# A hybrid decoder block on eight cores: barriers between four stages taken out, loads and first chunks of the next stage issued among the last steps of the one before

## The reference

```python
h = rmsnorm(x, attn_norm_g)
c_q, c_kv, k_pe, dq, dk, dv, ga, gb = split(h @ w_in)
o_a = mla_attention(c_q, c_kv, k_pe, ...) @ w_o_mla      # 8 heads, dense causal, low rank q and kv, RoPE
o_b = dilated_attention(dq, dk, dv) @ w_o_dil            # 3 groups (window, dilation) = (128,1),(512,4),(2048,16), 4 heads each
x = x + (sigmoid(ga + b_a) * o_a + sigmoid(gb + b_b) * o_b) @ w_out
h2 = rmsnorm(x, ffn_norm_g)
u = causal_dwconv(h2 @ w_up, conv_w, conv_b)             # width 3, 2 * 5504 features
x = x + (silu(u_gate) * u_up) @ w_down
out = rmsnorm(x, final_norm_g)
```

## Time and profile before

| | |
|---|---|
| median of 3 runs | 4726.3 us (4726.19 to 4990.38) |
| profiled execution | 4733.6 us, span of its slowest core (6) 4732.1 us |
| spans of the eight cores | 4712.8 to 4732.1 us |
| PE busy | 4335.3 us (92%) |
| VectorE, ACT busy | 1826.8 us (39%), 1532.8 us (32%) |
| DMA | 802 MB, mean 170 GB/s |

### The profile page before, as it was taken

The page is one execution under the profiler, slowest core; times in us unless marked ns, Lnnn a source line. Parts: engine busy times, 40 slices in busy tenths (PEclk is TensorE's granted clock), DMA queues, the critical chain, the costliest instruction groups (busy, mean ns, idle before and its releaser), DMA issues.

```text
span 4732.1 us, 79343 instructions; the slowest of 8 cores (4712.8 to 4732.1 us)
## 1 busy us (share of the span) xinstructions
PE 4335.3 (92%) x29258; PEld 2556.6 (54%) x29456; DVE 1826.8 (39%) x3318; ACT 1532.8 (32%) x2872; POOL 133.0 (3%) x223
## 2 busy tenths in 40 slices
PE   4979999964979899789999999999999999999998
PEld 3856666632545555445555555555555555555554
DVE  4733333200221322314752267224752267323762
ACT  3636666630111212213431244113431144113330
POOL 0000000000000000000000000000000000000000
PEclk8989999987989999789999999999999999999999
DMA  8648797889898442076556655676666655676555
GB/s 238 224 77 105 106 108 106 108 174 134 155 163 168 116 109 66 5 226 198 189 199 218 219 187 187 203 239 197 188 199 210 220 187 188 201 236 197 187 176 169
DMA packets 193662, 802.49 MB, mean 170 GB/s; under 512 B 23348, under 2 KB 44324, under 8 KB 177380
## 3 DMA queue, kind: packets, MB, share of 16 engines
q1 hardware_dynamic: 164148, 607.49, 40.1%
q0 software_dynamic: 29136, 189.92, 24.6%
HBM read 882.30 MB, written 138.96 MB: 216 GB/s over the span
## 4 chain that ended last, share of the span: by engine, by line
PE 84%; DMA 6%; DVE 3%; ACT 2%; issue 2%; another core or an unknown queue 2%; SPq 1%; DVEq 0%; POOL 0%; ACTq 0%; POOLq 0%
PE wide L260 76%; PE bank L260 7%; DMA cs<-cosT 2%; DMA h<-Hs 1%; DMA w<-w_gate_bf 1%; SPq L74 1%; ACT pt L269 1%; DVE tm L275 1%; DMA wuq<-w_uq 1%; DMA wd<-w_dn_bf 0%; ACT pt L536 0%; DVE zacc L272 0%; DVE on L484 0%; ACT zacc L269 0%
## 5 line engine op out<-in xcount | busy, mean ns | idle before, releaser
L260 PE MATMUL wide<-h,w 128*128 128x410 bf16 (+2 forms) x11297 | 2069.9, 341 | 161.9 <-DMA h<-Hs 149.6
L260 PEld LDWEIGHTS wide<-h,w 128*128 128x128 bf16 x11360 | 1094.4, 98 | 1091.9 <-issue 188.5
L260 PE MATMUL wide<-hid,wd 128*128 128x410 bf16 x3440 | 603.3, 336 | 1.4 <-DMA wd<-w_dn_bf 1.4
L275 DVE SCALAR_TENSOR_TENSOR ac<-u,vecs_sb,ac 128x410 f32<-128x410 f32 x860 | 551.5, 642 | 45.6 <-DVE ac L275 0.9
L269 ACT ACTIVATE ac<-u,vecs_sb 128x410 f32<-128x410 f32 x430 | 313.8, 730 | 539.9 <-DVE u L272 539.9
L260 PEld LDWEIGHTS wide<-hid,wd 128*128 128x128 bf16 x3440 | 334.8, 97 | 269.1 <-issue 2.2
L272 DVE TENSOR_TENSOR u<-wide,rs 128x410 f32<-128x410 f32 x430 | 251.0, 584 | 300.9 <-PE wide L260 244.5
L536 ACT ACTIVATE pt<-wide,vecs_sb 128x1024 bf16<-128x1024 f32 x256 | 284.4, 1114 | 211.9 <-PE wide L260 202.7
L269 ACT ACTIVATE sq<-x 128x410 f32<-128x410 f32 (+1 forms) x166 | 138.5, 834 | 554.6 <-DVE x L272 525.6
L260 PE MATMUL wide<-qp,kpe 128*128 128x512 bf16 (+4 forms) x953 | 306.4, 339 | 9.8 <-DVE vh L447 4.2
L272 DVE TENSOR_TENSOR x<-wide,x 128x410 f32<-128x410 f32 x160 | 93.5, 584 | 476.8 <-PE wide L260 476.8
(11 more groups left out here) (146 smaller groups left out, 3076.6 us busy)
## 6 DMA issues: line engine op xcount, KB each, us to landing
w<-w_up_bf SPq DMA_DIRECT2D x430, 512.0 KB, 3.4
w<-w_gate_bf SPq DMA_DIRECT2D x160, 512.0 KB, 4.1
h<-Hs SPq DMA_DIRECT2D x64, 1024.0 KB, 14.8
wd<-w_dn_bf SPq DMA_DIRECT2D x80, 704.0 KB, 4.3
wd<-w_dn_bf SPq DMA_DIRECT2D x80, 672.0 KB, 4.2
w_up_bf<-w_up POOLq DMA_DIRECT2D x43, 1024.0 KB, 13.9
w<-w_out_bf SPq DMA_DIRECT2D x80, 512.0 KB, 4.2
x<-xT SPq DMA_DIRECT2D x16, 2048.0 KB, 10.2
```

Source lines behind the costliest of these rows:

```text
L260: P.op("pe", lambda E: E.matmul(out_ap, lhsT=lhsT_ap, rhs=rhs_ap, start=start, stop=stop, **kw), reads=reads, writes=[out_T])
L275: P.op("dve", lambda E: E.scalar_tensor_tensor(out=out_ap, in0=in0, scalar=scalar, in1=in1, op0=op0, op1=op1), reads=reads, writes=[out_T])
```

## The change

The four stages become one phase: `end_phase` is called once, at the end. For that each SBUF tile gets a fixed place, and a "generation" (its stage). When a tile is first touched it waits for the readers and writers of those earlier tiles that lie where it lies (`touch`). Tensors in DRAM that one stage writes and another reads (`Hs`, `MOs` by head, the cast weights by name) are tracked too (`Dram`). Then work is moved:

- Stage 1: w_lat tiles 6, 4, 5 first; 0 to 3 one each after j = 0 to 3. Stage 2's wukv and its tables csq are sent at j = 13, wuq at j = 15. wukv and csq lie in free space, wuq in the place of x tile 1.
- Stage 2: the tails of stage 1's last chunk run after the first six of head 0's units. Fill also runs whenever the next product opens the output banks (`opens`). Casts: 68 here, not 63.
- Stage 3 becomes a generator that yields after each projection group. h tiles 0 and 1 and five weights are sent at the start of head 6, the bias table and four weights at that of head 7. Its first eight groups (j = 0 to 2) are head 7's fill, and one more runs with each pending step after head 7. Evictions of these use one bank (6), later three. Casts: two after each j from 3 on, 37 in all.
- Stage 4: mo is two tiles (heads of the latent attention, of the dilated one). Twelve gate groups (`gate`, `PRE`) are issued in pairs between the last seven steps of stage 3; h is sent before them. Gate outputs have 16 tiles, not 4. The rest is as before.

The functions of stage 3 (`chunk`, `quad`, `halo`, `finish`) move up in the file, with their text unchanged but for names. The core of the diff:

```diff
+    def touch(self, deps):
+        assert not self.dead, "tile used again where a later one lies: " + self.name
+        if not self.seen:
+            self.seen = True
+            for o in self.over:
+                o.dead = True
+                if o.lw is not None:
+                    deps.add(o.lw)
+                deps.update(o.rd)
...
+class Dram:
+    def __init__(self):
+        self.lws = []
+
+    def on_read(self, o, deps):
+        deps.update(self.lws)
+
+    def on_write(self, o, deps):
+        self.lws.append(o)
...
-            dst, src = casts[cast_i[0]]
-            P.dma("pool", dst.rearrange("a p m -> (a p) m"), src.rearrange("a p m -> (a p) m"), key="cast%d" % (cast_i[0] % 4),
-                  xdeps=[after])
+            dst, src, nm = casts[cast_i[0]]
+            P.dma("pool", dst.rearrange("a p m -> (a p) m"), src.rearrange("a p m -> (a p) m"), writes=[bf_M[nm]],
+                  key="cast_" + nm, xdeps=[after])
...
+    def T_at(name, t, lo, hi, gen):
+        over = [o for o in known if o.gen < gen and o.lo < hi and lo < o.hi]
+        n = T(name, t, lo, hi, gen, over)
+        known.append(n)
+        return n
...
+    la = Space(1, 3072, 44064)
...
+    s1 = Space(1, 60480, 212832)
...
+    s2 = Space(2, 44064, 143200)
...
+    s3z = Space(3, 143200, 212832)
+    w3 = [s3z("w3_%d" % i, [128, 16, 128], BF16) for i in range(5)]
+    hr3 = Ring([s3z("h3_%d" % i, [128, 16, 512], BF16) for i in range(3)])
+    s3a = Space(3, 3072, 44064)
...
+    NC, NT4, PRE = 410, 5, 12
+    w4 = [T_at("w4_%d" % i, t.t, t.lo, t.hi, 4) for i, t in enumerate(w3[0:7])]
+    s4 = Space(4, 163680, 180064)
+    sgr4 = Ring([s4("sg4_%d" % i, [128, NC], BF16) for i in range(PRE + 4)])
...
+    for i in (6, 4, 5):
+        wl_load(i)
...
+            if j < 4:
+                wl_load(j, [P.ops[-1]])
+            if j == NT1 - 3:
+                P.dma("pool", wukv_all.t[:], w_ukv_d.rearrange("o p (k m) -> p o k m", m=128), writes=[wukv_all], key="wukv")
+                P.dma("sp", csq.t[0:64, :], cos_d[:, HALO0:SEQ], writes=[csq], key="cosq")
+                P.dma("sp", csq.t[64:128, :], sin_d[:, HALO0:SEQ], writes=[csq], key="sinq")
+            if j == NT1 - 1:
+                P.dma("pool", wuq_all.t[:], w_uq_d.rearrange("o p (k m) -> p o k m", m=128), writes=[wuq_all], key="wuq")
...
+                    if j >= 3:
+                        cast_some(cast_i[0] + 2, P.ops[-1])
...
+        for u in units[0:6]:
+            u()
+        for f in older:
+            f()
+        for u in units[6:]:
             u()
...
+        ncast_p2 = len(casts) * 65 // 100
         for h in range(8):
             Kh, Vh, qn, qp = cur
-            nxt, fill = head_units(h + 1, Ring([banks[6]])) if h < 7 else (None, [])
+            if h < 7:
+                nxt, fill = head_units(h + 1, Ring([banks[6]]))
+            else:
+                nxt, fill = None, [lambda: next(gen3) for _ in range(8)]
+                load_bias()
+                for kg in WORDER[5:]:
+                    wt0[kg] = load_w(0, *kg)
+            if h == 6:
+                hts.extend([load_h(0), load_h(1)])
+                for kg in WORDER[0:5]:
+                    wt0[kg] = load_w(0, *kg)
+            nfill = len(fill)
             stepn, total = 0, 55
...
+                opens = len(pend) > LAG and pend[0][0]
+                if fill and (opens or len(fill) * total > nfill * (total - stepn)):
                     fill.pop(0)()
                 while len(pend) > LAG:
-                    pend.pop(0)()
+                    pend.pop(0)[1]()
...
+            pend.pop(0)[1]()
+            next(gen3)
...
+        pb3[0] = Ring(banks[4:7])
+        for _ in gen3:
+            pass
...
+        def load_mo(it):
+            for i, (a, b) in enumerate(((0, 8), (8, 12))):
+                P.dma("pool", mo.t[:, a:b, :], MOs[a:b, :, it * NC:(it + 1) * NC].rearrange("c p t -> p c t"),
+                      reads=MOs_M[a:b], writes=[moc[i]], key="mo4_%d" % i)
...
+        def gate(m, half):
+            wg, sg = wload("w_gate", 16 * half + m, 16), sgr.next()
+            b = linear(wg, 16, hsc, lambda kc: hs.t[:, kc, :])
+            act(sg, sg.t[:], b.t[:, 0:NC], AF.Sigmoid, [b, vecs], bias=vcol(V_BGATE + half * 16 + m))
+            return sg
...
+        load_h(0)
+        P.op("dve", lambda E: E.memset(ones_f.t[:], 1.0), writes=[ones_f])
+        P.op("dve", lambda E: E.memset(carry.t[:], 0.0), writes=[carry])
+        pre = []
+        run_steps()
+        while steps:
+            for _ in range(2):
+                if len(pre) < PRE:
+                    pre.append(gate(len(pre) // 2, len(pre) % 2))
+            run_steps()
+        while len(pre) < PRE:
+            pre.append(gate(len(pre) // 2, len(pre) % 2))
+        load_mo(0)
         load_x(0)
+        pb4[0] = Ring(banks[0:6])
         for it in range(NT4):
...
+                for half, (nm, kcn, mobase) in enumerate((("w_omla", 8, 0), ("w_odil", 4, 8))):
+                    sg, tm = pre.pop(0) if pre else gate(m, half), tmr.next()
+                    wo = wload(nm, m, kcn)
```

More of the change, by code:

```diff
@@ L201, in build_program @@
     MOs = dram("MOs", [12, 128, NEXT], BF16, "Internal")
-    Hs_T = T("Hs", None)
-    bf = {}
+    Hs_M = Dram()
+    MOs_M = [Dram() for _ in range(12)]
+    bf, bf_M = {}, {}
     casts = []
@@ L210, in build_program @@
         for i in range(0, n, step):
-            casts.append((bf[nm][i:min(i + step, n)], src[i:min(i + step, n)]))
+            casts.append((bf[nm][i:min(i + step, n)], src[i:min(i + step, n)], nm))
+        bf_M[nm] = Dram()
     cast_i = [0]
@@ new lines, in build_program @@
+    cqn = la("cqn", [128, 4, NEXT], BF16)
+    ckvn = la("ckvn", [128, 2, SEQ], BF16)
+    kpe = la("kpe", [128, SEQ], BF16)
+    s1 = Space(1, 60480, 212832)
+    x_1 = s1("x1_1", [128, 16, TW], F32)
+    sqr1 = Ring([s1("sq1_%d" % i, [128, 16, TW], BF16) for i in range(2)])
+    x_2 = s1("x1_2", [128, 16, TW], F32)
+    x_0 = s1("x1_0", [128, 16, TW], F32)
+    xr1 = Ring([x_0, x_1, x_2])
+    wl = [s1("wl%d" % i, [128, 16, 128], BF16) for i in range(7)]
+    raw1 = Ring([s1("raw1_%d" % i, [128, 4, TW], F32) for i in range(2)])
@@ new lines, in build_program @@
+    sqs1 = Ring([s1("sqs1_%d" % i, [128, 4, TW], BF16) for i in range(2)])
+    csr1 = Ring([s1("cs1_%d" % i, [128, TW], F32) for i in range(4)])
+    tmr1 = Ring([s1("tm1_%d" % i, [128, TW], F32) for i in range(2)])
+    rsr1 = Ring([s1("rs1_%d" % i, [128, TW], F32) for i in range(5)])
+    hr1 = Ring([s1("h1_%d" % i, [128, 16, TW], BF16) for i in range(4)])
+    VP = 136
+    s2 = Space(2, 44064, 143200)
+    wukv_all = s2("wukv", [128, 16, 2, 128], BF16)
+    csq = s2("csq", [128, NEXT], F32)
@@ new lines, in build_program @@
+    dor.append(s3c("dout1", [128, 1025], BF16))
+    dor = Ring(dor)
+    Uacc = s3c("uacc", [128, NEXT], F32)
+    Zacc = s3c("zacc", [128, NEXT], F32)
+    ptr3 = Ring([s3c("pt3_%d" % i, [128, 1024], BF16) for i in range(2)])
+    tmr3 = Ring([s3c("tm3_%d" % i, [128, 1024], F32) for i in range(2)])
+    qT += [s3c("dq%d" % g, [128, NEXT], BF16) for g in (1, 2)]
+    Vt += [s3c("vt1", [128, 20, 128], BF16), vt2]
+    qTj = [[part("dq%d_%d" % (g, j), qT[g]) for j in range(8)] for g in range(3)]
@@ new lines, in build_program @@
+    mo = s4("mo4", [128, 12, NC], BF16)
+    moc = [part("mo4a", mo), part("mo4b", mo)]
+    w4.append(s4("w4_7", [128, 16, 128], BF16))
+    wr4 = Ring(w4)
+    s4 = Space(4, 196448, 212832)
+    hs = s4("h4", [128, 16, NC], BF16)
+    hsc = [part("h4c%d" % k, hs) for k in range(16)]
+    carry = s4("carry4", [128, 86, 2], F32)
+    ones_f = s4("ones4", [128, 128], F32)
+    s4 = Space(4, 11264, 44064)
+    xs = s4("x4", [128, 16, NC], F32)
+    xsc = [part("x4c%d" % k, xs) for k in range(16)]
```

540 lines of the change are left out of this document (241 added, 299 removed).

## The result

The change makes the kernel faster by 2.3%: the ratio of the times after to before is 0.9774, with an interval of 0.9751 to 0.9798. Its executions took 4616.1 to 4622.7 us, against 4726.2 and 4726.3 before. By the ratio that is 107 us (95 to 118) where 196 were forecast, and the time lies above the range of 4480 to 4600.

A forecast was written before the change was run, and what follows sets the result against it. Bound: PE, nearly full in stage 4, with idle time elsewhere, including waits for h tiles. 6 + 23 + 12 + 108.5 + 28.7 - 16 + 34 = 196 us off the median 4726.3 gives 4530; range 4480 to 4600.

The forecast's parts named there:

- A: Start of stage 1: four w_lat loads moved later leave less before the first x; 6 us gain (0 to 12).
- B: Stage 1 to 2: wukv, csq and wuq sent early, query units start sooner; 23 us gain (20 to 30).
- C: Stage 2 output-bank openings: a fill unit of the next head covers PE's waits; 12 us gain (0 to 20).
- D: Stage 2 to 3 and slot s = 0: early loads and eight chunks in head 7; 108.5 us gain.
- Rival 3: Stage 2 to 3: something behind the barrier already held the order, tiles arrive no faster; 82 us off, 4644; chance 0.05.
- E: Stage 3 slot s = 1: fewer casts make it cost what s = 2 does; 28.7 us gain (20 to 32).
- G: Stage 3 to 4: twelve gate groups and one omla group done earlier; 34 us gain (21 to 36).
- F: Heads 6, 7 and s = 0: moved DMA work makes h tiles late; 16 us loss (0 to 60).
- sign of failure: Head 7 fill chunks wait for DMA, or h waits total over 60 us: where the forecast fails first.
- rival 4: Head 7: each of eight chunks waits 28 us behind casts, attention too; 225 us lost, slower at 4755; chance 0.03.
- Rival 1: Slot s = 0: the DMA debt is not paid, late h tiles cost 60 us; 109.5 off, 4617; chance 0.12.
- equal turns between queues: Engines alternate queues per packet: tiles beside casts take about twice their time, F nothing, sum 4514; as rival 4488, chance 0.08.

The follow-up runs named there:

- no_opens: The changed kernel without the extra fill unit where the output banks open; one run took 4613.2 us.
- os_on_pool: The changed kernel with the stores of the latent attention's outputs issued by POOL, not SP; ratio 0.9732, fastest run 4590.5 us.
- before_new_casts: The kernel before, barriers left in, with the cast plan of the changed kernel alone; ratio 0.9852, fastest 4652.6 us.
- spread_casts: The changed kernel with 48 casts by head 5's end, none in heads 6 and 7, then 10, 13, 17, 17 by slot; ratio 0.9634, fastest 4548.6 us.
- gates_behind: The changed kernel with sixteen gate groups, four behind the last output step, weights sent before the last stores, and another cast plan; ratio 0.9615, fastest 4536.2 us.
- no_casts_67: The changed kernel with 50 casts by head 5's end, none in heads 6 and 7, three after each j from 3; ratio 0.9676, fastest 4570.0 us.

## Why the prediction was right and wrong

**Right.** *A and B* were forecast at 29 us and brought 21 and 25 on cores 6 and 2 (18 and 29 on cores 0 and 4). The rows at 270.50 and 275.66 show that the tails of j = 15 pause PE for 2.1 and 3.9 us; no wait for wukv or wuq is left. *C* was 12; the waits of no_opens put it at 11. *D*, behind stage 2: s = 0 was to cost from j = 3 on what s = 2 costs, 161.7 us. To the marks of the table, which leave out about 7 us of that stretch, it is 153.9 and 154.3, 97% of it busy. Rival 3 (what stood behind the barrier holds the order anyway) is out. The chunks in stage 2 cost about what was charged, 25.7 us for ten at a price of 30.2. *E* was 28.7 and is 31.2 (core 6), and s = 1, 2 and 3 agree within 3 us. *G* goes as it was told, with a wait between the last output step and the first `mo` group. It was to be 20 us to the first `odil` group; it was 24.7 (1917.99 to 1942.70). The `omla` group that was to run in between itself came 18.2 us late: its tile stands behind the stores on SP, and the forecast had not followed SP's list to it. In size G is smaller than told: 25.6 us on core 6 and 11 to 24 on the other cores read, for 34.

**Wrong: F, the DMA debt.** It was to cost 16 us, as late h tiles in s = 0. That engines would be full from head 6 on was right (0.98 to 1.00). But s = 0 came out clean, and the price was paid in stage 2, at 72 to 82 us. By steps:

- Heads 6 and 7, up to the first transposes of stage 3: 249.3 us on core 6 and 252.6 on core 2, and 194.7 without casts there. These 55 and 58 us are the debt itself, counted at 25 to 30 us of engine time and priced at 16. Part of it is the term "the last stores of head 7 stand on SP behind an h load, 3 more", priced as the landing of one store at the end. Every query block of heads 6 and 7 stores through SP, an h half kept SP for 12 to 26 us on core 2, and only three os tiles stand between. os_on_pool puts this term at 17 to 20 us, net of what it gives back.
- The forecast never asked what 68 casts instead of 63 do to heads 0 to 5. It counted engine time, of which they had some to spare (a share of 0.80). Heads 1 to 5 lost 17 us (core 6) and 24 (core 2) against 84.5 each, the length of a head that is left alone. In before_new_casts the same casts cost 11 to 26 us in all of stage 2.

Together this is 72 us on core 6 and 82 on core 2. Less the 16 that F had, 56 and 66 are left; the line "these two together" of the table misses by 55 and 73.

The prediction's own sign of failure, a fill chunk of head 7 that waits for DMA, came on every core read: one wait of 7 to 22 us. It is the mechanism of rival 4 at a small part of its price.

Rival 1 (debt not paid, -60) had nearly the right time (4617) and nearly the right sum for F, but by luck: it put the loss in s = 0, and its reason, PE waiting for late h tiles, makes 22.0 us on core 2.

Of equal turns between queues: SP's issues lasting 12 to 26 us a half speak against the assumption that a load of two halves beside casts only takes twice its 7.7 us of work. Which share of the engines each queue got was not measured. The Trainium skill says in "DMA: Bandwidth & Descriptors", section "Issuing engines are not separate DMA queues", that issuing on several engines only saves the time to issue, "which is usually small relative to the DMA itself". In head 7 this time was the loss: with the same transfers and another issuer for the stores, it went from 121.9 to 144.1 us down to 88.2 to 92.4, though only 17 to 20 us of that were left at the start of stage 3.

**What the change is worth by its parts.** The cast plan alone brings 70 us with the barriers in; the barriers' removal, the moved loads and the chunks bring 37 more as written. With the casts placed anew the whole is worth more: by their ratios spread_casts is 173 us under before and gates_behind 182. No run has that cast plan with the barriers left in, so how much of it is the plan's alone is open, and that it comes near the forecast 196 does not make the forecast right.

## What to carry to other kernels

When transfers are moved ahead into a busy stage, ask of each queue what already stands in it there, and multiply by the time that one issue takes with the DMA engines full, not by the time when they are idle. A store whose tile comes from a short ring should not stand behind a large prefetch; but moving it helps little while the engines stay full. And when a barrier goes, plan the background copies anew: here spread_casts, which moves nothing but casts, is worth 66 us by the ratios against the kernel as changed, and its head 7 takes 88.2 us with the stores still on SP.

## What the hardware showed

- One issue of a 1 MB half on SP took 1.2 to 2.9 us in a stretch with a mean DMA share of 0.37 (no_casts_67, head 7) and 12 to 26 us at 0.98 to 1.00 (after). Small weight loads at the crossing took 0.32 us.
- PE paused for up to 4.8 us (os_on_pool) with no wait that the profile shows. Between 305 and 800 us these pauses are 9 to 18 us on a core of after, 4 to 10 in before_new_casts, 0 to 2 in spread_casts. The reason is open.
- ACT loaded a table eleven times between Exp and Sigmoid, and once more for Ln, at 1.28 us each in the crossing, and PE did not wait for it once, as the gate pairs cover it.
